# Two-layer encoder with grouped MoE: one expert load moved ahead of a wait, two matmul products swapped

## The reference

```python
def _moe(h, router_w, w_gate, w_up, w_down):
    probs = softmax(x @ router_w)                  # 16 experts in 4 groups
    top_v, top_i = lax.top_k(probs.reshape(T, 4, 4), 2)
    g_sel = argmax(sum(top_v, -1), -1)             # one group a token, two experts in it
    ...
    def expert_block(args):                        # for each block of tokens of one expert
        xblk, e = args
        hid = jax.nn.silu(xblk @ w_gate[e]) * (xblk @ w_up[e])
        return hid @ w_down[e]
    ...
    y = zeros.at[buf_tok].add(yb * buf_gate[:, None])
```

## Time and profile before

| | us |
|---|---|
| median of 3 runs | 1343.64 |
| lowest and highest run | 1342.66, 1345.62 |
| the profiled execution, its own time | 1340.68 |
| its span in the profile | 1338.8 |
| mean granted TensorE clock | 0.973 |

### The profile page before, as it was taken

How to read it: one execution, slowest core, us unless ns; L and a number is a source line. 1 busy time by engine, 2 the same in 40 slices (tenths; PEclk the granted TensorE clock), 3 DMA queues, 4 the chain that set the end, 5 groups by cost and what they waited for, 6 DMA issues and landing times.

```text
span 1338.8 us, 13921 instructions
## 1 busy us (share of the span) xinstructions
PE 1250.3 (93%) x5523; PEld 583.1 (44%) x5523; DVE 519.9 (39%) x1010; ACT 186.1 (14%) x313; POOL 166.6 (12%) x126
## 2 busy tenths in 40 slices
PE   8999989988999898699999999999899899989984
PEld 4444455543333333244456555565446333333332
DVE  2254753471211110430356666566725622111108
ACT  0025500110000000011211111111112100000000
POOL 0000500013000000200022323223300220000011
PEclk9999989999999999899999999999999989999997
DMA  9920073269999997743320222200064699999974
GB/s 357 379 88 1 11 303 133 88 244 363 416 425 428 417 432 318 287 110 97 121 60 5 63 63 63 63 0 0 0 269 192 268 401 410 429 424 421 426 276 158
DMA packets 82832, 301.51 MB, mean 225 GB/s; under 512 B 6388, under 2 KB 50776, under 8 KB 70360
## 3 DMA queue, kind: packets, MB, share of 16 engines
q1 hardware_dynamic: 61296, 262.55, 49.6%
q10 hardware_dynamic: 16872, 21.38, 4.4%
q0 software_dynamic: 4608, 16.78, 3.3%
HBM read 269.23 MB, written 31.46 MB: 225 GB/s over the span
## 4 chain that ended last, share of the span: by engine, by line
PE 65%; DMA 13%; issue 12%; DVE 6%; POOL 3%; ACT 0%; DVEq 0%; SPq 0%; POOLq 0%
PE ps L606 15%; PE ps L772 14%; PE ps L478 8%; PE ps L641 7%; DMA W<-moe_w_up 4%; PE ps L759 4%; DMA S<-moe_w_up 4%; PE ps L794 4%; PE ps L555 4%; PE ps L824 2%; DMA slot_rows<-hT 1%; DVE S L1639 1%; PE ps L591 1%; POOL slot_rows L1736 1%; PE ps L812 1%
## 5 line engine op out<-in xcount | busy, mean ns | idle before, releaser
L606 PE MATMUL ps<-W,S 128*32 128x512 f32 (+1 forms) x1344 | 286.3, 605 | 17.3 <-DMA W<-moe_w_up 8.7
L772 PE MATMUL ps<-hT,W 128*128 128x512 f32 x512 | 232.5, 593 | 0.7 <-ACT W L903 0.7
L606 PE MATMUL ps<-S 128*64 128x512 f32 (+1 forms) x448 | 200.1, 604 | 0.0
L606 PEld LDWEIGHTS ps<-W,S 128*32 128x32 f32 (+1 forms) x1344 | 87.2, 121 | 153.8 <-issue 150.5
L641 PE MATMUL ps<-W,hT 128*32 128x512 f32 (+1 forms) x672 | 144.9, 602 | 6.9 <-issue 6.0
L772 PEld LDWEIGHTS ps<-hT,W 128*128 128x128 f32 x512 | 92.8, 191 | 90.4 <-issue 88.5
L641 PE MATMUL ps<-S,hT 128*64 128x512 f32 (+1 forms) x224 | 100.7, 603 | 1.0 <-DMA W<-moe_w_down 1.0
L1770 POOL TENSOR_TENSOR W<-S,sq 128x256 f32<-128x256 f32 x64 | 73.5, 1148 | 159.3 <-PE ps L794 115.6
L903 ACT ACTIVATE hT<-ps 128x512 f32<-128x512 f32 x68 | 39.0, 598 | 364.7 <-PE ps L641 262.1
L478 PE MATMUL ps<-W,hT 128*128 128x512 f32 x192 | 83.5, 593 | 1.6 <-DMA W<-w_in_even 1.6
L606 PEld LDWEIGHTS ps<-S 128*64 128x64 f32 (+1 forms) x448 | 57.4, 131 | 44.0 <-issue 43.2
(11 more groups left out here) (260 smaller groups left out, 1316.1 us busy)
## 6 DMA issues: line engine op xcount, KB each, us to landing
W<-moe_w_gate SPq DMA_DIRECT2D x22, 2048.0 KB, 14.7
W<-moe_w_up SPq DMA_DIRECT2D x22, 2048.0 KB, 14.6
W<-moe_w_down SPq DMA_DIRECT2D x22, 2048.0 KB, 16.2
S<-moe_w_gate SPq DMA_DIRECT2D x10, 2048.0 KB, 13.5
S<-moe_w_up SPq DMA_DIRECT2D x10, 2048.0 KB, 17.8
S<-moe_w_down SPq DMA_DIRECT2D x10, 2048.0 KB, 14.7
W<-w_in_odd SPq DMA_DIRECT2D x32, 512.0 KB, 6.4
slot_rows<-S ACTq DMA_DIRECT2D x4, 2816.0 KB, 20.2
```

Of the source, the lines that this page charges most:

```text
L606: last = pe.matmul(ps[a:a + n, bank, :], xgT[:, c, a:a + n], w[L][slot_of(p)][:, c, :], start=(c == 0), stop=(c == ND - 1))
L772: last = pe.matmul(ps[:, f % 2, :], ring[slot][:, f, c, :], hT[:, c, :], start=(c == 0), stop=(c == ND - 1))
```

## The change

1. SP (`moe_loads`). Before, SP waits for `scattered`, issues the row loads of units 1 and 2, waits for the expert table, waits for unit 0's gate product and then issues place 3's gate piece. Now it waits for the table and unit 0's gate product first, issues place 3's gate piece, and only then waits for `scattered` and issues the two row loads.
2. PE (`moe`). The down product of unit 8 now stands ahead of the gate product of unit 9.
3. ScalarE. The copies and the store of unit 8 stand ahead of the sigmoid of unit 9, as they now must.
4. POOL. In layer 0 the gathers of tiles 2 and 3 write over the slot that holds place 15's gate piece, so POOL waits for unit 9's gate product before the gather of tile 2.

```diff
             def moe_loads(L):
 
-                sp.wait_ge(scattered, (L + 1) * 16 * 2 * NT)
-                for k in (1, 2):
-                    load_rows(L, k, k)
                 sp.wait_ge(table_done, 2 * L + 1)
                 expert_at = {}
                 for u in range(NU):
@@ -359,6 +356,10 @@
                         sp.wait_ge(gate_mm[L], u + 1)
                     for p in freed:
                         load_gate(L, expert_at[p], slot_of(p))
+                    if u == 0:
+                        sp.wait_ge(scattered, (L + 1) * 16 * 2 * NT)
+                        for k in (1, 2):
+                            load_rows(L, k, k)
                     if freed:
                         sp.wait_ge(up_mm[L], u + 1)
                     for p in freed:
@@ -681,8 +682,8 @@
                         router_sums(1, 7)
                     if L == 0 and u == 7:
                         router_spread(1, 7)
+                down(LAST - 1)
                 gate(LAST)
-                down(LAST - 1)
                 up(LAST)
@@ -1043,9 +1044,11 @@
                 store(1, 1)
-                for u in range(3, NU):
+                for u in range(3, LAST):
                     sigmoid(u)
                     store(u - 1, (u - 1) % 2, 16 * ((u - 1) // 2))
+                store(LAST - 1, (LAST - 1) % 2, 16 * ((LAST - 1) // 2))
+                sigmoid(LAST)
@@ -1744,6 +1747,8 @@
                 for t in range(NT):
+                    if t == 2 and L == 0:
+                        pool.wait_ge(gate_mm[L], NU)
                     for k in range(2):
```

## The result

| | before | after |
|---|---|---|
| median, us | 1343.7 (4 runs, 1342.66 to 1345.62) | 1360.36 (4 runs, 1359.5 to 1361.47) |
| ratio, 95% interval | | 1.0123 [1.0105, 1.014] |
| profiled execution, its span, us | 1340.68, 1338.8 | 1359.5, 1357.7 |
| mean granted TensorE clock | 0.973 | 0.967 |

The change makes the kernel 16.7 us slower. I had forecast slower, by 8.55 us; the size is twice that and outside the range (1343.6 to 1355.3).

The account below looks back on a forecast made before the run. It took a ring of PE freeing slots and the full load queue as the bound. Place 4's lateness, 4.0 + 4.15, plus 2 x 0.2 for the clock gave +8.55 us: 1352.2 us against the median, range 1343.6 to 1355.3.

Parts of the forecast that it names:

- The rows' delay: At unit 1's rows, each layer: the early gate load sharing DMA with the scatter delays them 4.3 us, range 1.2 to 4.9.
- the lower bound's mechanism: At unit 1's rows: the scatter keeps its pace, rows only stand behind the gate load on SP's queue, 1.2 us late.
- my sign of a wrong forecast: At the scatter's end in layer 0: the forecast is wrong if the scatter lands near 309 all the same.
- The cold start in layer 0: At unit 1's rows in layer 0: PE begins cold after the longer wait, making place 4's load issue 1.05 us later.
- Place 4's landing: Place 4's gate load lands 8.15 us after issue, after a DMA dip: 4.0 us later in layer 0, 4.15 in layer 1.
- PE had waited 2.17 us there: At unit 4's up product, layer 0: PE's 5.35 us lateness shrinks to 3.2, the queue's 4.0 counts and stays.
- The swap: At unit 8's down product: it runs colder after a 10 us wait, +0.2 us a layer, bounds -0.3 and +0.9.
- Covered, by 2 us: At layer 1's end: unit 9 ends 7.0 us later, but PE's add still finishes 2 us before VectorE wants it.
- unit 8's down product starts no earlier: It starts when place 13's down piece lands in either order, since that piece's issue is not moved.
- layer 0 hides the late unit 9: At layer 0's end: gathers land later still, beside the big load, so unit 9 ending 7.0 us later costs nothing.
- The rows are hardly delayed: Rival at unit 1's rows: the scatter keeps its pace, queue place costs 1.2 us; 1345.6 us, 17 in 100.
- The stream starts earlier and stays ahead: Rival on the load queue: every landing comes 4.8 us forward in each layer; 1334.0 us, 9 in 100.

Follow-up runs that it names:

- group 2: Kernel before and changed kernel, both unedited, run again beside each other and other kernels on another chip; the changed kernel took 1.0129 of before, +17.3 us.
- The first pair: First comparison: kernel before against the changed kernel with all edits; medians 1343.7 and 1360.36 us, ratio 1.0123.
- part 1 alone: Only the SP edit (place 3's gate load ahead of the scatter wait) against the kernel before; 1.0118, 1.0101 and, in the fifth group, 1.0083.
- before again: The kernel before, no edit, run and profiled again on another chip beside the changed kernel; median 1341.8 us in that group.
- part 2 alone: Only the PE, ScalarE and POOL edits (unit 8's down product before unit 9's gate product) against the kernel before; 1.0053, +7.1 us.

## Why the prediction was wrong in size

**The rows' delay (4.3 us, bounds 1.2 and 4.9): mechanism right, mis-sized.** On the first chip the rows came 6.1 us later in layer 0 and 7.6 in layer 1, above the upper bound. I had let the load take at most its own 4.9 us at 425 GB/s. Side by side the two moved 359 GB/s, less than the scatter alone (370) or a load alone (425), here in a window of the changed kernel, columns as in the earlier trace rows:

```profile
303.00:313.00 10.00, 5.70 (x56) 1.50 (x48) 0.90 (x2) 0.00 (x0) 0.96 (x2) 0.90 1.00 359
```

My estimate from this: 2.10 MB at 359 GB/s are 5.8 us, close to the 6.1 in layer 0. On the chip of group 2 the delay was 4.1 and 3.2 us, near the forecast, but that is luck: it came by the lower bound's mechanism, the place on the queue, with the scatter untouched. The scatter landing on time was even my sign of a wrong forecast, and the kernel was as slow. There the queue place alone costs 4.2 us, not the 1.2 that I gave it, since the load was issued only 2 us before the scatter's end and not 7. The Trainium skill (DMA: Bandwidth & Descriptors, "Queues, rings and completion order") has the engines go round their queues packet by packet. The first pair agrees that both transfers go on together and both are held up: the load took 10.9 us to land where one alone takes 8.0, and the scatter ended 6.1 us later. How the packets' sizes divide the engines, no run here shows.

**The cold start in layer 0 (1.05 us): right.** 1.97 instead of 1.34 us for the turn; 11.4 us from the turn to place 4's gate load instead of 10.4. On the chips where the kernel before waited at most 1.1 us at the rows, both layers lose it, 1.7 to 2.1 us each (9.4 us from the turn to place 4's gate load before, 11.1 and 11.5 with part 1 alone).

**Place 4's landing (8.15 us after its issue, a dip before it): right.** 8.0 us, and the DMA stood still from 326 to 331.

**"PE had waited 2.17 us there, so it would be ready 3.2 us late; the queue is 4.0 us late, and the larger counts. From there on the queue is full in both kernels, and what it is late stays": this step failed.** It takes the wait at unit 4 as slack of PE, and place 4's landing as the last place where lateness is made. Landings (issue and time to landing added), layer 0 / 1:

| us after the scatter's first issue | place 4's gate | place 6's up | place 4's down | unit 4's up |
|---|---|---|---|---|
| before again | 36.3 / 37.0 | 68.9 / 70.1 | 75.1 / 76.0 | 97.1 / 98.0 |
| part 1 alone (group 5) | 40.5 / 40.5 | 73.8 / 74.0 | 81.2 / 80.1 | 103.3 / 102.2 |
| before | 38.5 / 37.5 | 71.4 / 70.8 | 77.5 / 78.2 | 99.2 / 100.1 |
| after | 44.4 / 44.0 | 77.7 / 77.2 | 85.5 / 84.9 | 107.6 / 106.9 |

With part 1 alone place 4's gate load lands 4.2 and 3.5 us late, near the 4.0 and 4.15 of my sum. But the load that ends the wait at unit 4 lands 6.2 and 4.2 us late, and the layers end 6.8 and 4.5 us late. So the lateness grew on the way from place 4 to unit 4, in layer 0 up to all that PE was late at the issue (6.0 us), and from unit 4 on it nearly stayed. In the changed kernel 5.9 and 6.5 us became 8.4 and 6.8. PE's wait at unit 4 was no slack: its load is issued when unit 3's up product ends, 375.65 before and 382.60 after, from the rows' turn to there PE waits for no load in either kernel, and the wait is as long as before or longer (3.2 us, 2.2 before), since the load came later too.

Nor is the queue full all the way to unit 4. Place 4's down piece lands 11.7 us after its issue at 368.0, only 3.7 more than into an empty queue; in the kernel before it was 11.0. The windows behind that issue, in the changed kernel:

```profile
368.00:372.00 4.00, 4.00 (x20) 1.68 (x22) 0.69 (x1) 0.60 (x1) 0.00 (x0) 1.00 0.96 336
372.00:376.00 4.00, 4.00 (x22) 1.34 (x20) 0.00 (x0) 0.26 (x1) 0.00 (x0) 1.00 0.97 369
```

This is where layer 0's lateness grows (6.3 to 8.0 us between place 6's up and place 4's down piece; 4.9 to 6.1 with part 1 alone). In the kernel before only one window of 4 us is low there, 352 GB/s from 360 to 364. That the late issue is what lowers the rate is my reading; no run tests it, and layer 1 grew much less.

**The swap (+0.2 a layer, bounds -0.3 and +0.9): mis-sized.** I priced the clock from a product that takes 8.80 us after a 3 us wait and a bound of 2.7 us lost. After 9 to 10 us it takes 8.4 to 9.7 us, so up to 2.7 lost is about right as the bound. What I took as certain was the 8.80 before; it is sometimes 7.10. "Covered, by 2 us" held for PE's adding of unit 9, which I had looked at, but not for VectorE's own steps of unit 9 and for the gathers, which I had not: layer 1's end takes 0.7 to 1.8 us longer. Measured, part 2 costs 7.1 us; of these the profiles show 1.6 to 3.3 in the products and 0.7 to 1.8 at the end. In the profile of part 2 alone unit 8's down product also starts 0.4 and 1.6 us later after the scatter's first issue than in the kernel before again; why, I can't say. Right were that unit 8's down product starts no earlier, that it stands behind a wait near 10 us, and that layer 0 hides the late unit 9 (from store to first norm 35.4 us in both kernels).

**The rivals.** "The rows are hardly delayed" fell with the 315.32; its mechanism, an undisturbed scatter, was there in group 2, but the place on the queue cost 4.2 us and not 1.2. "The stream starts earlier and stays ahead" fell with the empty 326 to 331: what was loaded early came back as a hole.

## What to carry to other kernels

In a ring where PE frees a slot, a load fills it and PE waits for it, don't count PE's wait for the load as slack: first look when that load was issued, and by whom. Where it was PE's own step, lateness went through here nearly whole. A load put ahead of a smaller one on which PE waits cost its own bytes here, whether it shared the engines or stood ahead on the queue, and the head start was worth nothing, since the queue ran dry behind it. Moving work out of a wait cost the clock of what followed; moving work into a wait (a down product ahead of an up product) was the only change here that gained. And when a unit is moved later, every engine that has a step in it ends later, not only the one on the chain.

## What was not expected of the hardware

The same unchanged code ran in two ways at one place. ScalarE's row for the end of unit 0's gate product, in the kernel before again, where the scatter's first issue is at 295.1:

```profile
306.76 0.60 ACT L1020 ACTIVATE hT<-ps 128x512 f32<-128x512 f32 x1 [10.17 <-remote]
```

It is 302.04 in the earlier trace rows, with the scatter's first issue at 294.6. The windows of PE in that stretch (length, PE busy, clock, DMA share, GB/s) have a slow place at full granted clock, here in the kernel before again:

```profile
300.00:303.00 3.00, 3.00 (x32) 1.00 0.95 373
303.00:306.00 3.00, 2.64 (x14) 1.00 0.98 384
```

In the first profile of the kernel before, the window from 303 to 306 has 32 matmuls as well. So PE loses some 4 us beside the scatter on some executions and not on others, in layer 0 as in layer 1. All profiles of one group go the same way, whatever their kernel, and the kernel before is found on both sides, so the kernel's code is not the cause. What is, no experiment here separates.
